# Moving the GELU of the compressed keys and values ahead of VectorE's weight split in its slot

## The reference

```python
def compress_blocks(kv, pos, w1, w2):
    """kv (B,G,S,dh) -> compressed (B,G,Nc,dh); block i covers [i*d, i*d+l)."""
    b, g, s, dh = kv.shape
    chunks = kv.reshape(b, g, s // CMP_STRIDE, CMP_STRIDE, dh)
    blocks = jnp.concatenate([chunks[:, :, :-1], chunks[:, :, 1:]], axis=3)
    blocks = (blocks + pos).reshape(b, g, blocks.shape[2], CMP_BLOCK * dh)
    return jax.nn.gelu(blocks @ w1) @ w2
...
    kc = rms_norm_2(compress_blocks(k_c, cmp_pos[0], cmp_w1[0], cmp_w2[0]), nsa_qk_norm[1])
    vc = compress_blocks(v_c, cmp_pos[1], cmp_w1[1], cmp_w2[1])
```

## Time and profile before

| | |
|---|---|
| time, median of 3 runs | 926.21 us (925.57 to 930.45) |
| profiled execution, its own time | 928.86 us |
| its span, first to last instruction | 927.1 us |
| mean granted TensorE clock | 0.996 |
| busy: TensorE, VectorE, ScalarE, GpSimd | 912.1, 619.0, 518.4, 76.2 us |
| DMA | 155.35 MB, mean 168 GB/s |

### The profile page before, as it was taken

One profiled execution on the slowest core, in us unless ns is written; L12 is line 12 of the kernel. 1 busy time (PEld: TensorE's weight loads), 2 busy tenths in 40 slices (PEclk: granted clock), 3 DMA queues, 4 the chain that ended last, 5 costly groups with the idle time before them and its releaser, 6 DMA issues.

```text
span 927.1 us, 14321 instructions
## 1 busy us (share of the span) xinstructions
PE 912.1 (98%) x5800; PEld 809.6 (87%) x5800; DVE 619.0 (67%) x789; ACT 518.4 (56%) x728; POOL 76.2 (8%) x145
## 2 busy tenths in 40 slices
PE   8999999999999999999999999999999899999998
PEld 7997888999988888888899887889999788888887
DVE  6535576766776665556677887888877576565664
ACT  6546666665455444444577775877374554444441
POOL 8502332020010000000000000000000000000000
PEclk9999999999999999999999998999999999999999
DMA  9654333476545555555545743443436365555551
GB/s 277 203 183 141 132 115 112 137 242 203 182 142 180 183 189 196 198 194 199 197 140 174 236 137 92 137 137 103 132 132 211 107 214 194 182 181 185 184 175 46
DMA packets 115672, 155.35 MB, mean 168 GB/s; under 512 B 2649, under 2 KB 94913, under 8 KB 115618
## 3 DMA queue, kind: packets, MB, share of 16 engines
q1 hardware_dynamic: 114704, 151.57, 50.4%
q0 software_dynamic: 864, 2.98, 0.9%
q10 hardware_dynamic: 50, 0.04, 0.0%
HBM read 153.53 MB, written 1.05 MB: 167 GB/s over the span
## 4 chain that ended last, share of the span: by engine, by line
PE 91%; DVE 4%; ACT 3%; issue 1%; DMA 1%; SPq 0%; ACTq 0%; DVEq 0%
PE PS L602 19%; PE PS L604 19%; PE PS L603 19%; PE PS L929 15%; PE PS L931 8%; DVE wlo L1792 1%; ACT whi L1232 1%; PE PS L1062 1%; PE PS L831 1%; PE PS L1040 1%; PE PS L974 1%; PE PS L783 1%; PE PS L717 1%; DVE hT L1876 1%; DMA res<-in_x_dram 1%
## 5 line engine op out<-in xcount | busy, mean ns | idle before, releaser
L1792 DVE TENSOR_TENSOR wlo<-raw,whi 128x2048 fp32r<-128x2048 f32 x140 | 321.5, 2297 | 145.9 <-ACT whi L1232 145.7
L1232 ACT CAST whi<-raw 128x2048 fp32r<-128x2048 f32 x141 | 268.6, 1905 | 110.6 <-PE PS L604 110.0
L929 PE MATMUL PS<-hT,whi 128*128 128x512 f32 x608 | 216.3, 399 | 1.9 <-DVE hT L1876 1.9
L602 PE MATMUL PS<-hT,whi 128*128 128x256 f32 (+1 forms) x616 | 177.9, 289 | 1.2 <-DVE hT L1876 1.0
L603 PE MATMUL PS<-hT,whi 128*128 128x256 f32 (+1 forms) x616 | 174.8, 284 | 0.0
L604 PE MATMUL PS<-hT,wlo 128*128 128x256 f32 (+1 forms) x616 | 174.8, 284 | 0.0
L931 PE MATMUL PS<-hT,wlo 128*128 128x256 f32 x608 | 170.7, 281 | 0.0
L929 PEld LDWEIGHTS PS<-hT,whi 128*128 128x128 f32 x608 | 114.2, 188 | 30.8 <-issue 1.7
L602 PEld LDWEIGHTS PS<-hT,whi 128*128 128x128 f32 (+1 forms) x616 | 118.3, 192 | 2.7 <-issue 1.2
L603 PEld LDWEIGHTS PS<-hT,whi 128*128 128x128 f32 (+1 forms) x616 | 118.2, 192 | 0.2
L604 PEld LDWEIGHTS PS<-hT,wlo 128*128 128x128 f32 (+1 forms) x616 | 118.2, 192 | 0.0
(11 more groups left out here) (361 smaller groups left out, 1259.7 us busy)
## 6 DMA issues: line engine op xcount, KB each, us to landing
raw<-in_w_in_dram SPq DMA_DIRECT2D x47, 1024.0 KB, 5.2
raw<-in_w_ff_dram SPq DMA_DIRECT2D x32, 1024.0 KB, 5.2
raw<-in_w_gate_dram SPq DMA_DIRECT2D x11, 1024.0 KB, 5.3
raw<-in_w_up_dram SPq DMA_DIRECT2D x11, 1024.0 KB, 5.3
raw<-in_w_down_dram SPq DMA_DIRECT2D x11, 1024.0 KB, 4.9
raw<-in_w_out_dram SPq DMA_DIRECT2D x8, 1024.0 KB, 4.9
raw<-in_w_proj_gla_dram SPq DMA_DIRECT2D x4, 1024.0 KB, 5.7
raw<-in_w_mem_kv_dram SPq DMA_DIRECT2D x4, 1024.0 KB, 5.1
```

The lines of the kernel that those rows point to most:

```text
L602: pe.matmul(dst, a_hi, b_hi, start=start, stop=False, skip_group_check=True)
L929: pe.matmul(PS[:, bank + c, :], w_hi[:, k, f], hT[:, k, :, :].rearrange("p w t -> p (w t)"), start=k == 0, stop=False, skip_group_check=True)
L1232: act.copy(whi[:, n % RING, :], raw[:, n % RING, :]).then_inc(hi_made, 1)
L1792: dve.tensor_tensor(wlo[:, n % RING, :], raw[:, n % RING, :], whi[:, n % RING, :].bitcast(F32), ALU.subtract).then_inc(lo_made, 1)
```

## The change

In VectorE's pass of a slot, both parts of the GELU are placed ahead of `split_lo(n + RING)` instead of behind it and behind `evac2_end`. The instructions, their operands and their semaphores are the same; no other engine's program changes.

```diff
@@ -2260,6 +2260,22 @@
                 if name == "vm0":
                     turned_lo(3, hT_hi, hT_lo, G_MIX2)
+                if s in (7, 11):
+
+                    b = int(s == 11)
+                    dve.wait_ge(h_raw, b + 1)
+                    link(dve.tensor_tensor(hwork, hid[b], hid[b], ALU.mult))
+                    link(dve.tensor_scalar(hwork, hwork, 0.044715, 1.0, ALU.mult, ALU.add))
+                    link(dve.tensor_tensor(hwork, hwork, hid[b], ALU.mult))
+
+                    dve.tensor_scalar(hwork, hwork, -50.0, None, ALU.max).then_inc(h_arg, 1)
+                if s in (8, 12):
+                    b = int(s == 12)
+                    dve.wait_ge(h_exp, b + 1)
+                    link(dve.tensor_scalar(hwork, hwork, 1.0, None, ALU.add))
+                    link(dve.reciprocal(hwork, hwork))
+                    dve.tensor_tensor(hid[b], hid[b], hwork, ALU.mult).then_inc(h_made, 1)
+                    dve.wait_ge(h_made, b + 1)
                 split_lo(n + RING)
                 if name[0] != "o":
                     evac2_end(name)
@@ -2288,22 +2304,6 @@
...
-                if s in (7, 11):
-
-                    b = int(s == 11)
-                    dve.wait_ge(h_raw, b + 1)
...
-                if s in (8, 12):
-                    b = int(s == 12)
-                    dve.wait_ge(h_exp, b + 1)
...
```

## The result

The changed kernel takes 923.11 us (median of 18 runs, 922.69 to 924.00), the kernel before 927.46 us (18 runs, 925.57 to 930.45). The ratio is 0.9949 with a 95% interval of 0.9939 to 0.9959: faster by half a per cent, by more than its uncertainty. The profiled execution went from 928.86 to 922.91 us, its span from 927.1 to 921.2.

The account below looks back on a forecast made before the run. TensorE was taken as the bound, busy 912.1 of 927.1 us, with two waits for VectorE's GELU. The sum was 928.86 - 0.79 - 2.04 - 2.95 = 923.08, say 923.1 us, range 919.8 to 926.4.

Parts of the forecast that it names:

- The step behind slot 14: TensorE was to reach the end of slot 14 earlier by 5.78 us, the sum of all three terms.
- First wait: TensorE's 1.45 us wait at line 1147 goes, the wait at line 1040 grows to 1.30 us, and 0.79 us stays.
- Second wait: TensorE's wait before line 1154 for the GELU in slot 12 goes whole: 2.04 us, with 0.78 us of margin.
- The clock: The 1.2 GHz stretch behind the wait before line 1154 does not come: 2.54 + 0.41 = 2.95 us, or 0 otherwise.
- no such stretch: The median run of the kernel before, 926.21 us, was thought to have no stretch at low clock, whose price is 2.95 us.
- shorter waits leave the clock alone: The low clock was said to follow only the 2.04 us wait, not the 1.5 us ones at lines 929 and 1147.
- the earlier argument counts in slot 8: ScalarE gets the exponential's argument near 521.1 instead of 523.2, so VectorE's 0.56 us wait for the cast goes.
- Rival 1: The profiled execution is slow for another reason and the usual run has the low clock too: 920.4 us, chance 0.15.
- Rival 2: The low clock stays or moves, for instance to the wait in slot 10: 926.0 us, chance 0.13.
- a stretch at another place: Sign against the prediction: a stretch at granted clock 0.50 standing somewhere else after the change.
- rival 3: VectorE is the real bound from slot 12 on, only 0.79 us stays: 928.1 us at most, chance 0.09.
- rival 4: The four delayed splits, 3.88 us in all, go to the end if chunks are taken at once: 932.7 us, chance 0.05.

Follow-up runs that it names:

- Experiment 4: The kernel before with ten small matmuls of the identity, result unread, inside the wait before line 1154: 926.55 us, ratio 0.9979.
- experiment 1: The kernel before, unchanged, run again to see each run with its own granted clock: 927.53 us, ratio 0.9994.
- experiment 2: Against the changed kernel, only the keys' two GELU parts (slots 7 and 8) ahead of the split, the values' behind it: 928.25 us, ratio 0.9990.
- experiment 3: Against the changed kernel, only the values' two GELU parts (slots 11 and 12) ahead of the split, the keys' behind it: 924.43 us, ratio 0.9953.
- experiment 5: The kernel before with unread small matmuls inside both waits, ten ahead of line 1154 and seven ahead of line 1147: 926.40 us, ratio 0.9973.
- experiment 6: Against the changed kernel, only the GELU's second parts (slots 8 and 12) ahead of the split, the first parts behind it: 922.72 us, ratio 0.9951.
- experiment 7: Against the changed kernel, only the GELU's first parts (slots 7 and 11) ahead of the split, the second parts behind it: 928.29 us, ratio 1.0002.
- experiment 9: The changed kernel with some 1.15 us of idle VectorE multiplications ahead of the split of slot 12: 922.80 us, ratio 0.9953.

## Why the prediction was right

**The time.** 923.1 was forecast, 923.11 measured, and the profiled execution gave 922.91 where the sum, made for one like it, had 923.08. That the median agrees to a hundredth is luck: the runs of the changed kernel at full clock alone spread from 922.69 to 923.16. The step behind slot 14 can be read directly: TensorE's line 997 comes there at 564.38 after 570.35 before, 5.97 us earlier, where the sum had 5.78.

**First wait, 0.79 us.** The wait at line 1147 went whole and half of it came back at line 1040, as said (1.37 us against the 1.30 worked out). Line 1040 came 0.90 us earlier, and 0.98 against the neighbouring work, since the matmuls of slot 9 end 0.08 us later in this execution (the last starts at 527.00, before at 526.92). The sum was 0.1 to 0.2 short because it subtracted VectorE's idle times as printed. In the rows its instructions overlap by some 0.1 us where none waits (the split of 525.95 with its 2.29 us ends at 528.24, the next instruction starts at 528.15), so that a wait that goes is worth a little more than its idle time.

**Second wait, 2.04 us.** Right. The result was due 0.78 us ahead of TensorE; in the trace after VectorE has gone on to its split at 555.90 and line 1154 starts at 556.61, 0.71 us later.

**The clock, 2.95 us.** Right for an execution like the profiled one: line 1154 gave back the 0.41 us taken for it, the stretch behind it ran at 1.00, and 10.73 - 7.77 = 2.96 us are gone between lines 1154 and 997. Experiment 4 shows that idle time of TensorE is the cause and not the lateness of the result. Whether the small matmuls behind this wait have a part in it was not tested. The section of the Trainium skill cited in the prediction, "Why this matters for your kernels" in "TensorE: Matmul & The Clock Gate", warns only of longer gaps; the trace and these runs, with 0.50 granted behind waits of 1.45 to 2.04 us, disagree with it.

**Where it failed.** Three statements behind the right number did not hold. First, that the median run had no such stretch: only 15 of 81 executions of the kernel before kept the full clock, and the median of its 18 runs beside the changed kernel, 927.46 us, lies in the group at 0.998, for which experiment 1 shows a stretch of half the length and a price of 1.50 us. That error sat in the baseline and not in the forecast time, which is why the measured gain is 4.35 us and not the 3.1 between 926.21 and 923.1; that 926.21 was so near the full-clock times was the luck of three runs. Second, that shorter waits leave the clock alone: true in one trace, not in those of experiments 2 to 5. Third, that the earlier argument counts in slot 8, because it ends VectorE's wait of 0.56 us for the cast: experiment 6 shows that the second part, put into that wait, does it alone, and 7 that the first part alone is worth half a microsecond of wait at most and nothing in the median.

**The rivals.** Rival 1, a low clock in the usual run, was right in its premise for most runs of the kernel before, but its time of 920.4 took the whole price off 926.21, a time that hardly held any of it. Rival 2 did not happen for the large stretch. Six of 18 runs still have a lowered clock, at a place that is not known; the prediction counted a stretch at another place as a sign against it, and for these runs that sign may hold. Rivals 3 and 4, VectorE as the bound and the delayed splits, fall with experiment 9 (1.1 us more on VectorE in slot 12 costs nothing), and rival 4 also with the list of waits, which names no `wlo` in slots 7 to 15. In slot 8 VectorE does bind, through the exponentials; that is the 1.37 us that is left.

## What to carry to other kernels

Small work whose result another engine wants soon does not belong behind a large instruction that has slots of lead: look for the wait in the busiest engine's list, read what its releaser did just before, and check how far ahead of its use that large instruction is. A chain worked out on one engine has to be closed through the others before a gain is booked. And where runs of one kernel spread, sort them by granted clock before comparing medians: three runs of a kernel with groups of 926, 927, 929 and 930 us say little of its median.

## What the runs showed of the hardware

TensorE's clock fell from the 2.4 to the 1.2 GHz level after idle times of 2.04 us, and of 1.45 to 1.50 us (experiments 2 to 5), in some executions of the same program and not in others. The stretches were 3.4 or 6.8 us long. In the thirteen profiles of this case each of them begins near the end of one of these waits, from 0.1 us before it to some 2.4 us behind it, but for one at the very end of the kernel, 2 us behind TensorE's last matmul (experiment 9). The mean clock was below 1.000 in 66 of 81 executions of the kernel before, with its waits of 1.45, 0.64 and 2.04 us in slots 9 to 13, and in 6 of 18 of the changed one, with 1.37 us alone there; part of either can come from the waits elsewhere.

Matmuls of no use in the waits took most of it away: in experiments 4 and 5, 15 of 24 runs are at 1.000 and none is under 0.998. What they cost at full clock is small. In the trace of experiment 4 they outlast the wait by 0.13 us; the full-clock median of experiment 5, 926.35 us, lies within the 925.84 to 926.66 of the kernel before beside it.

The price of the clock is not small beside the waits: the medians of the groups lie 1.45, 3.2 and 4.4 us above that of the full clock, where the whole change is worth 2.72 us at full clock.
